# Setup of a two-layer encoder kernel taken apart by token halves, with idle turns on TensorE

## What is computed

```python
def ffn_half(x, g_pre, g_post, w_gu, w_dn):          # d_ff = 2816
    gate, up = split(rmsnorm(x, g_pre) @ w_gu)
    return x + 0.5 * rmsnorm((silu(gate) * up) @ w_dn, g_post)

for l in range(2):
    x = ffn_half(x, g[0], g[1], w_ffn_gu[l, 0], w_ffn_dn[l, 0])
    u = rmsnorm(x, g[2])
    # one input projection, then band attention (8 heads x 64, learned clipped
    # relative-position bias) and differential attention (4 heads, ALiBi)
    x = x + rmsnorm(concat(band(u @ w_in[l]), diff(u @ w_in[l])) @ w_out[l], g[3])
    x = x + rmsnorm(cross_attend(rmsnorm(x, g[4]) @ w_cq[l], mem) @ w_co[l], g[5])
    x = ffn_half(x, g[6], g[7], w_ffn_gu[l, 1], w_ffn_dn[l, 1])
# returned: x of prompt and sample, and the new keys and values of each layer
```

## Time and profile before

| | us |
|---|---|
| median of 3 timed runs | 2567.17 |
| lowest and highest | 2567.15, 2569.9 |
| profiled execution, its own time | 2569.76 |
| its span, first instruction to last | 2568.0 |

### The profile page before, as it was taken

How to read it: one execution, slowest core, us unless ns; L and a number is a source line. 1 busy time by engine, 2 the same in 40 slices (tenths; PEclk the granted TensorE clock), 3 DMA queues, 4 the chain that set the end, 5 groups by cost and what they waited for, 6 DMA issues and landing times.

```text
span 2568.0 us, 47241 instructions
## 1 busy us (share of the span) xinstructions
PE 2499.1 (97%) x19325; PEld 2400.7 (93%) x19325; DVE 1209.4 (47%) x2059; ACT 911.0 (35%) x1650; POOL 23.8 (1%) x55
## 2 busy tenths in 40 slices
PE   7999999999899999999999999999998999999998
PEld 6999999997599899999999999999966989999998
DVE  5444325435747644442364443254467567444324
ACT  4222324224745632222242222242256545222221
POOL 1000000000000000000000000000000000000000
PEclk9999999999999999999999999999999999999999
DMA  6332332433033123233323233333321322232331
GB/s 185 90 90 82 97 91 67 141 100 118 17 95 111 47 85 90 85 96 91 89 67 89 83 90 94 87 108 117 114 71 41 108 67 73 83 90 84 98 89 60
DMA packets 384734, 229.81 MB, mean 89 GB/s; under 512 B 6892, under 2 KB 371454, under 8 KB 384608
## 3 DMA queue, kind: packets, MB, share of 16 engines
q1 hardware_dynamic: 379040, 206.66, 27.2%
q0 software_dynamic: 4368, 16.92, 1.9%
q10 hardware_dynamic: 1200, 4.46, 0.5%
HBM read 214.46 MB, written 18.79 MB: 91 GB/s over the span
## 4 chain that ended last, share of the span: by engine, by line
PE 91%; DVE 5%; ACT 2%; DMA 1%; issue 1%; DVEq 0%; SPq 0%; ACTq 0%
PE psum L675 77%; PE psum L650 4%; PE psum L995 3%; PE psum L733 2%; PE psum L1027 2%; PE psum L688 1%; DVE x L1604 1%; PE psum L1009 1%; DVE u_lo L1555 1%; DMA w_raw<-in_w_ffn_gu 1%; DVE w_lo L1560 0%; ACT w_hi L1210 0%; DVE y_mix L1601 0%; DMA w_raw<-in_w_ckv 0%; DVE y_ffn L1601 0%
## 5 line engine op out<-in xcount | busy, mean ns | idle before, releaser
L675 PE MATMUL psum<-u_hi,w_hi 128*128 128x272 f32 x3840 | 809.3, 290 | 8.6 <-ACT w_hi L1210 3.8
L675 PE MATMUL psum<-u_lo,w_hi 128*128 128x272 f32 x3840 | 804.2, 288 | 0.0
L1210 ACT ACTIVATE w_hi<-w_raw 128x1024 fp32r<-128x1024 f32 (+1 forms) x326 | 365.3, 1122 | 1067.1 <-PE psum L675 1030.8
L675 PEld LDWEIGHTS psum<-u_hi,w_hi 128*128 128x128 f32 x3840 | 607.5, 188 | 12.6 <-ACT w_hi L1210 3.9
L675 PEld LDWEIGHTS psum<-u_lo,w_hi 128*128 128x128 f32 x3840 | 605.3, 188 | 0.0
L1560 DVE TENSOR_TENSOR w_lo<-w_raw,w_hi 128x1024 fp32r<-128x1024 f32 (+1 forms) x326 | 424.2, 1302 | 310.7 <-ACT w_hi L1210 310.6
L675 PE MATMUL psum<-u_hi,w_lo 128*128 128x272 f32 x3840 | 544.3, 289 | 0.0
L675 PEld LDWEIGHTS psum<-u_hi,w_lo 128*128 128x128 f32 x3840 | 506.7, 189 | 0.0
L675 PE MATMUL psum<-h_hi,w_hi 128*128 128x272 f32 x1408 | 301.3, 289 | 0.0
L675 PE MATMUL psum<-h_lo,w_hi 128*128 128x272 f32 x1408 | 300.6, 289 | 0.0
L675 PEld LDWEIGHTS psum<-h_hi,w_hi 128*128 128x128 f32 x1408 | 227.5, 189 | 0.0
(11 more groups left out here) (250 smaller groups left out, 2211.7 us busy)
## 6 DMA issues: line engine op xcount, KB each, us to landing
w_raw<-in_w_ffn_gu SPq DMA_DIRECT2D x176, 512.0 KB, 3.8
w_raw<-in_w_ffn_dn SPq DMA_DIRECT2D x64, 704.0 KB, 4.5
w_raw<-in_w_in SPq DMA_DIRECT2D x48, 512.0 KB, 3.8
w_raw<-in_w_out SPq DMA_DIRECT2D x16, 512.0 KB, 3.7
w_raw<-in_w_ckv SPq DMA_DIRECT2D x16, 512.0 KB, 3.6
bias_tab_dram<-bias_rev_dram POOLq DMA_DIRECT2D x1, 5120.0 KB, 22.5
out<-k_nat POOLq DMA_DIRECT2D x4, 1024.0 KB, 5.0
out<-v_nat POOLq DMA_DIRECT2D x4, 1024.0 KB, 5.8
```

The lines of the kernel that those rows point to most:

```text
L675: pe_last[0] = pe.matmul(psum[:, bank + part, 0:c1 - c0], weight[:, slot, b * 128:(b + 1) * 128], xs[:, c0:c1], start=start, stop=stop)
L1210: return act.activation(out, src, ACT.Copy, scale=scale)
```

## The change

Loads of x: six pieces instead of two, on two queues. SP issues tokens 0:128, the memory norm's gains, tokens 256:272, then the first weight tile, tokens 400:512, then the second weight tile. ACT issues the norm gains, tokens 128:256, tokens 272:400, and the sample tokens in two parts of 16. The tokens that don't fill 128 (256:272 and half of the sample) share a tile that DVE first clears.

Turning: PE first turns `ones`, a constant tile, into a bank that nobody reads, 20 times; then the gains, 8 more idle turns, then half A in eight blocks of three turns with an idle turn behind each. Half B is turned inside `first_chunks`: three blocks behind the first sweep, five behind the second. `x_first` counts the copied blocks of half A, `x_ready` those of half B. DVE's and ACT's queues are rewritten to match: gains and x copies first, constants behind the u_lo. The first product of the second pair waits for `setup_vals`.

Bias tables: eight transfers of two tables, each behind the landing of one more load of slot 1, from the third on.

```diff
+        sp.dma_start(x_nat[:, 0, :], x_prompt[0, 0:128, :]).then_inc(x_loaded[0], 16)
+        sp.dma_start(gains_nat[16:18, :], mem_norm_g).then_inc(gains_loaded, 16)
+        sp.wait_ge(rem_cleared, 1)
+        sp.dma_start(x_nat[0:16, NT, :], x_prompt[0, 256:H, :]).then_inc(rem_loaded, 16)
+        load(0, 0, w_gu_v[0][:, :, 0:128], first=True)
+        sp.dma_start(x_nat[0:112, 3, :], x_prompt[0, H + 128:SEQ, :]).then_inc(x_loaded[3], 16)
+        load(0, 1, w_gu_v[0][:, :, DFF:DFF + 128], first=True)
...
+        for t in range(0, 16, 2):
+            pool.wait_ge(w_loaded[1], 16 * (t // 2 + 3))
+            pool.dma_start(tab_dram[t:t + 2], bass.AP(rev_dram.tensor, 768 * t + 127, [[768, 2], [-1, 128], [1, TABW]])
+                           ).then_inc(tab_made, 16)
...
+        def keep_busy(times):
+            for _ in range(times):
+                turn(psum[:, 0, 0:128], ones[:, :])
+        def turn_x(half, ks):
+            for k in ks:
+                bank, d = X_BANK[half][k], slice(k * 128, k * 128 + 128)
+                if half == 0 and k >= 6:
+                    pe.wait_ge(x_first, k - 5)
+                if half and k < 3:
+                    pe.wait_ge(x_first, (3, 7, 8)[k])
+                if half and k >= 3:
+                    pe.wait_ge(x_ready, k - 2)
+                if half == 0:
+                    turn(psum[:, bank, 0:128], x_nat[:, 0, d])
+                    turn(psum[:, bank, 128:256], x_nat[:, 1, d])
+                    turn(psum[:, bank, 256:384], x_nat[:, NT, d]).then_inc(x_turned, 1)
+                    keep_busy(1)
+                else:
+                    turn(psum[:, bank, 240:368], x_nat[:, NT, d])
+                    turn(psum[:, bank, 0:128], x_nat[:, 2, d])
+                    turn(psum[:, bank, 128:256], x_nat[:, 3, d]).then_inc(x_turned, 1)
...
+        keep_busy(20)
+        pe.wait_ge(gains_loaded, 32)
+        for k in range(KD):
+            mm = turn(psum[:, 4, k * 18:(k + 1) * 18], gains_nat[:, k * 128:(k + 1) * 128])
+        mm.then_inc(gains_turned, 1)
+        keep_busy(8)
+        pe.wait_ge(x_loaded[0], 16)
+        pe.wait_ge(x_loaded[1], 16)
+        pe.wait_ge(rem_loaded, 32)
+        turn_x(0, range(KD))
```

More of the change, by code:

```diff
@@ L1033, in _ @@
         pe.wait_ge(iden, 2)
-        pe.wait_ge(consts, 4)
[L1035 to L1048, removed]
+        pe.wait_ge(consts, 1)
+        keep_busy(20)
[8 more added lines that the diff above has]
+        turn_x(0, range(KD))
+        pe.wait_ge(consts, 4)
         for l in range(DEPTH):
@@ L1261, in high @@
         def high(q, half, k, gain):
-            act.wait_ge(x_ready, 8 * q + (4 * half + k // 2 + 1 if q else k + 1))
+            if q:
+                act.wait_ge(x_ready, 8 * q + 4 * half + k // 2 + 1)
+            else:
+                act.wait_ge((x_first, x_ready)[half], k + 1)
             cols = half_of(half)
@@ L1267, in square_x @@
         def square_x(q, half, p):
-            act.wait_ge(x_ready, 8 * q + (4 * half + p + 1 if q else 2 * p + 2))
+            if q:
+                act.wait_ge(x_ready, 8 * q + 4 * half + p + 1)
+            else:
+                act.wait_ge((x_first, x_ready)[half], 2 * p + 2)
             cols = half_of(half)
@@ L1418, in scale_table @@
             copy(table[:, h % 2, :], dist[:, :], scale=-SLOPES[h]).then_inc(tab_scaled, 1)
[L1421 to L1424, removed]
+        act.dma_start(gains_nat[0:16, :], norm_g.rearrange("l i d -> (l i) d")).then_inc(gains_loaded, 16)
+        act.dma_start(x_nat[:, 1, :], x_prompt[0, 128:256, :]).then_inc(x_loaded[1], 16)
+        act.dma_start(x_nat[:, 2, :], x_prompt[0, H:H + 128, :]).then_inc(x_loaded[2], 16)
+        act.dma_start(x_nat[112:128, 3, :], x_sample[0, 0:16, :]).then_inc(x_loaded[3], 16)
+        act.wait_ge(rem_cleared, 1)
+        act.dma_start(x_nat[16:SAMPLE, NT, :], x_sample[0, 16:SAMPLE, :]).then_inc(rem_loaded, 16)
+        act.wait_ge(consts, 2)
+        warm(ACT.Copy)
+        act.wait_ge(layer_gains, 1)
+        for k in range(7):
+            high(0, 0, k, 8)
+        cut_hi(0, 0, first=True)
+        high(0, 0, 7, 8)
+        for k in range(6):
+            high(0, 1, k, 8)
+        cut_hi(0, 1, first=True)
+        for k in range(6, KD):
+            high(0, 1, k, 8)
+        for half in range(2):
+            for p in range(4):
+                square_x(0, half, p)
         act.wait_ge(dist_ready, 1)
@@ L1817, in keep_values @@
                               ALU.mult).then_inc(o_kept, 1)
-        for s in range(2):
-            cut_lo(0, s)
+        dve.memset(x_nat[:, NT, :], 0.0).then_inc(rem_cleared, 1)
+        dve.wait_ge(gains_turned, 1)
+        dve.tensor_copy(gains_all[:, :, :], psum[:, 4, 0:KD * 18].rearrange("p (k n) -> p k n", k=KD)).then_inc(setup_vals, 1)
+        dve.wait_ge(setup_vals, 1)
+        dve.tensor_copy(gains[:, :, 8:9], gains_all[:, :, 0:1]).then_inc(layer_gains, 1)
+        for k in range(KD):
+            dve.wait_ge(x_turned, k + 1)
+            dve.tensor_copy(x[:, k, 0:H], psum[:, X_BANK[0][k], 0:H]).then_inc(x_first, 1)
+        cut_lo(0, 0)
+        for k in range(KD):
+            dve.wait_ge(x_turned, KD + k + 1)
+            dve.tensor_copy(x[:, k, H:T], psum[:, X_BANK[1][k], 0:H]).then_inc(x_ready, 1)
+        cut_lo(0, 1)
+        dve.wait_ge(layer_gains, 1)
+        for half in range(2):
+            for k in range(KD):
+                low(0, half, k, 8)
         dve.memset(headsq[:, :], 1.0).then_inc(setup_done, 1)
-        dve.wait_ge(setup_loaded, 80)
-        dve.tensor_copy(bias_rev[:, 511:767], bias_in[:, 256:0:-1]).then_inc(rev_ready, 1)
-        dve.tensor_copy(bias_rev[:, 0:511], bias_in[:, 256:257].broadcast_to([16, 511])).then_inc(rev_ready, 1)
+        dve.wait_ge(setup_loaded, 48)
         for n in range(2 * DEPTH):
```

48 lines of the change are left out of this document (21 added, 27 removed).

## The result

| | us |
|---|---|
| changed kernel, median of 4 runs | 2598.58 (2596.38 to 2598.83) |
| kernel before, median of 4 runs | 2568.53 (2567.15 to 2570.36) |
| ratio | 1.0114, 95% interval 1.01 to 1.0127 |
| profiled execution of the changed kernel, its span | 2597.0 |

The change makes the kernel 1.1% slower, 30 us. The prediction was 2557.0 with a range up to 2563.5, and 0.04 for slower. Where the time went shows in a ledger: ACT cuts 326 weight tiles in a fixed order, so the start of the nth cut in one trace can be subtracted from the same cut in the other. I count from 0; cut 2 is the first of the second pair.

The account below looks back on a forecast made before the run. PE, busy 97% of 2568.0 us, was taken as the bound, the change worth what it takes off the 43.87 us before the second pair. Second pair at 33.7, gain 10.2: 2567.17 - 10.2 = 2557.0 us, range 2553.0 to 2563.5.

Parts of the forecast that it names:

- Table transfers: Eight pieces of 640 KB beside weight loads: 2.8 us each, 6.6 of 9.55 us with a load, costed at nothing.
- Rival E: Table pieces hold up weight loads: at 12 us a load, eight waits of 2.4, 19 us, 2576; chance 0.04.
- Step 1: Setup, start of half A's turns: x loaded at 8.1 us, PE's own queue until 8.5, taken as 8.4.
- rival D: Loads decide: half A's last x lands at 12.2 instead of 8.4, clock low; 1.9 us off, 2565.3; chance 0.08.
- Step 2: Setup, until the first weight is cut: 13.8 us at high clock, 16.4 at low, 14.9 in the mixed forecast.
- Step 3: First products and half B's turns: second cut done at 20.0 us (high clock), 26.1 (low), 23.0 (mixed forecast).
- rival B: Setup: the clock stays up from half A on; 13.2 us off, 2554.0; chance 0.18.
- Step 4: From the second weight cut to the second pair of weight columns: 10.7 us, waiting for setup_vals taken as 0.
- Which clock: Setup: clock up from turning alone at about 11 us, down before the first product, up again at 19.6.
- forecast A: Setup with mixed clock, raised by turning alone: second pair at 33.7 us, 10.2 off, 2557.0; chance 0.52.
- rival C: Setup: turning doesn't raise the clock; order and halves alone give 5.7 us off, 2561.5; chance 0.18.
- signs of being wrong: Second pair after 39 us, x landing after 10, or PE waiting for a DMA-delayed w_hi between 50 and 160 us.

Follow-up runs that it names:

- t7: t1 with the last piece of half A's x issued ahead of half B's on ACT's queue; 2558.27 us, ratio 0.9966.
- t5: t1 without any idle turn; 2560.45 us, ratio 0.9968.
- t10: t7 without any idle turn; 2557.68 us, ratio 0.9958.
- t8: t1 with 36 idle turns instead of 8 behind the gains; 2559.94 us.
- t1: Changed kernel with each of the eight table transfers taking 16 rows of all sixteen tables instead of two whole tables; 2562.88 us, ratio 0.9977.
- t9: t7 with 16 and 4 idle turns in place of 20 and 8; 2559.19 us, ratio 0.9959.
- t2: Changed kernel with four table transfers of four tables instead of eight of two; 2578.53 us.
- t3: Changed kernel with the table made by one transfer of all sixteen tables, as in the kernel before; 2568.66 us, ratio 1.0002.

## Why the prediction was wrong

**The step that failed** is the one headed "Table transfers", with "2.8 us each if they go at that pace" and "so I cost them at nothing". The pace was that of the 5 MB transfer, taken per byte. But that one has sixteen tables outermost and kept all engines busy, a piece of the change has two: it took 16.9. The cover, 9.55 us for a load, was worked out rightly and was gone at 15.1. Rival E had the mechanism (pieces hold up loads), the place and the point of decision; it took 12 us for such a load, 2.4 of wait and 19 in all, against 15.1, 5.5 a round and 37. Its 0.04 rested on "it needs three times the slowdown of the sum", that is, on the same price per byte; and three times is for its 12 us, while its own point of decision, 9.55, needs 5.75 us more than a load's 3.8, twice the 2.8 of the sum.

What the loss consists of: the page's costliest group of products, before and after (count, busy us, mean ns, idle time ahead and what ended most of it):

```profile
L675 PE MATMUL psum<-u_hi,w_hi 128*128 128x272 f32 x3840 | 809.3, 290 | 8.6 <-ACT w_hi L1210 3.8
```

```profile
L683 PE MATMUL psum<-u_hi,w_hi 128*128 128x272 f32 x3840 | 817.0, 292 | 33.1 <-ACT w_hi L1250 28.3
```

24.5 us of it are idle time of PE. The rest, 12.5, goes with a clock that fell at most of the holes: between 80 and 193 us it was at 0.50 in six stretches, 27 us in all, which costs up to half of that. From 101 to 104 us for example:

```profile
101.00:104.00 3.00, 3.00 (x15) 3.00 (x14) 3.00 (x4) 1.69 (x3) 0.00 (x0) 0.50 0.39 45
```

That slower pace is no second cause, as I read it: loads set the round of 17.6 us, and it fills time in which PE would have stood idle.

**Step 1, mis-sized.** The first turn of x was forecast at 8.4, bound by PE's own queue; it came at 10.74, bound by DMA. The queues from 2 to 10.8 us of the changed kernel:

```profile
q1 hardware_dynamic: 1170, 1.09, 44.6%
q10 hardware_dynamic: 384, 1.25, 41.3%
q0 software_dynamic: 144, 0.28, 12.3%
```

The sum had 1.85 MB in that time (1.2, then 0.65 on ACT's queue alone); 2.62 MB were moved, since SP's queue went on with 1.09 and not 0.58, and POOL's 0.28 were left out. 2.62 MB at the 345 GB/s of the earlier trace rows from 2.2 on is 9.8; it landed at 10.6. This is rival D in kind, in a good half of its size: D priced x at 12.2, 3.8 late, and it was 2.3. t7 confirms the term: with that piece first, x comes before PE is ready.

**Step 2, right in kind.** First cut done at 18.2, forecast 14.9. Of the 3.3 late, 2.3 are step 1, the rest that the clock rose at 15.5 and not "at about 11 us", a moment for which the prediction had no row.

**Step 3.** I expected the clock to fall again in the hole ahead of the first product. It didn't (8 products in 1.22, 9 turns in 1.15), so about 1.6 of the 3.3 came back: second cut done 24.65, forecast 23.0. Here rival B was right, and not by a rule that could have been read beforehand: in t5 and t10 the clock did fall near a hole of that length (see the end).

**Step 4.** Forecast 10.7 from there to the second pair, measured 10.95, and no wait for `setup_vals`: PE's 0.31 us is for the weight. Second pair at 35.60 against 33.7, a gain of 8.3 against 10.2.

**Which clock.** Turning alone raised it: forecast A over rival C, in the trace of the change and in t8. But the price of that, "the idle turns", was nearly nought as built (t1 against t5), since PE stopped turning 3.35 us before x came.

**Numbers.** With the tables priced as I did, 2568.5 - 8.3 gives 2560.2. t1, which has just that, is at 2562.88 and within the range; its interval, 3.3 to 8.2 us off, holds the setup's 7.9 near its edge. Of the prediction's own signs of being wrong two came true: x landed after 10, at 10.6, and PE waited for a w_hi that waited for DMA, seven times and 24.3 us in all.

## What to carry to other kernels

Price a transfer by the engines that it is spread over, not by its bytes: read its outermost dimension on both sides. With 2 and with 4 outermost its packets stood on 2 and on 4 engines here, and a load that shared those engines waited packet for packet. When a large transfer is cut up to make room for others, cut along an inner dimension, and price the loads that run beside a piece, not only the piece. Before adding work that keeps a clock up, look what it waits for: it must last until the data are there, and an order of issue that brings the data sooner was worth more here (3.75 us against 2.6 for the longer filling, one execution each).

The fastest kernels of this study, t7, t9 and t10, are 0.34 to 0.42% faster than the one before (9 to 10 us), and about 1.5% faster than the change as it was made; t5, at 0.32%, can't be told from them by its interval.

## What the runs showed of the hardware

- A DRAM-to-DRAM transfer with 2, 4 and 16 tables outermost kept a share of 0.13, 0.25 and 1.00 of the DMA engines busy, at 52, 103 and 318 GB/s (loads beside it included).
- Two queues with work on the same DMA engines took turns packet for packet, though one had packets of 512 bytes and the other of 5 KB: 37 against 38 in the change (76 to 80 us), 73 against 73 in t2 (76 to 80), 410 against 409 in t3 (48 to 56). A load beside 64 long packets per engine takes about 15 us (15.1 in the change, 15.4 to 15.7 in t2; 9.2, 19.4 and 15.1 in t3, where two of the three shared the queue), and beside 8 of them 4.9, where a load alone takes 3.8 (t1, the load issued at 84.04 and the one before it).
- Transposes alone raised TensorE's clock, between the 20 from 1.57 (0.21 apart) and the eight at 6.30 (0.11 apart) in the change, and in t8. With the same 28 turns ahead, t7's eight at 6.99 were still slow. In t5 and t10, which have no idle turns, it rose at 13.7 and 12.0, while x was turned. Why the moment differs between executions stays open.
- The length of a hole ahead of the first product didn't tell what the clock did: it stayed at 1.00 through 1.54 us in the change and 2.66 in t9, and fell to 0.50 at 17.2 in t5 and at 15.4 in t10, soon after holes of 1.92 and 1.84.
- Whole times scatter by more than the setups differ. After cut 60 t5 lost 2.8 us and t9 3.4, while t7 gained 1.5; mean granted clocks were 0.991, 0.990 and 0.993. The times go with the clock, but what makes it fall late in the kernel wasn't looked into.
